# A stick-breaking mask moved from TensorE to VectorE, and an earlier release of an output copy, in a two-block transformer kernel

## The chip, the cores and the metric

The kernel runs on one core of a Trainium2 chip. The metric is the device time of one execution in microseconds. Below, the engines go by their names or by the profile's short forms: TensorE (PE; PEld is its weight load), VectorE (DVE), ScalarE (ACT), GpSimd (POOL), SyncE (SP).

## What is computed

A sequence of 512 tokens of width 1024 goes through two layers of a first block and then two layers of a second block, all in float32. The change lies in the second block, whose layer mixes four attention kinds: sliding window, latent (MLA), stick-breaking and forgetting (FoX) attention. The stick-breaking part of the reference, for which the mask is needed:

```python
z = jnp.einsum('bqhd,bkhd->bhqk', qi, k).astype(jnp.float32) * scale
strict = kpos[None, :] < qpos[:, None]
log_1mb = jnp.where(strict, jax.nn.log_sigmoid(-z), 0.0)
between = lax.cumsum(log_1mb, axis=3, reverse=True) - log_1mb
a = jnp.where(strict, jnp.exp(jax.nn.log_sigmoid(z) + between), 0.0)
return jnp.einsum('bhqk,bkhd->bqhd', a.astype(v.dtype), v)
```

After it each of the four groups is scaled by its root mean square and multiplied by the output weights:

```python
xf = mix.astype(jnp.float32).reshape(B, S, N_GROUPS, GROUP_WIDTH)
xf = xf * lax.rsqrt(jnp.mean(jnp.square(xf), axis=-1, keepdims=True) + eps)
y = _group_rmsnorm(mix, mix_g[l]) @ w_o[l]
```

## The kernel before

Every large product is made of three matmuls on numbers split into a high and a low part (mm3, L503 to L505), with moving tiles of 512 columns. Weights come from HBM in units of 128x1024; ScalarE casts the high part (L969), VectorE subtracts the low part (L977), both some units ahead of TensorE.

The attention of a layer of block 2 (tensor_block2, scalar_block2, vector_block2) runs in 32 steps. Step number 4a + j belongs to the pair of heads a (0 to 7) and its block j of 128 positions. The kinds are KIND = sliding window for a = 0, 1, latent for 2, 3, stick-breaking (SB) for 4, 5 and forgetting for 6, 7; so steps 16 to 23 are stick-breaking. A pair's two heads are m = 0 and 1. The order of the work is written out by hand, each engine with its own loop over the steps, and semaphores between them.

TensorE, step s: scores of s; weighted sum over V of step s-2; a filling of the projections' matmuls (nine at these steps); "between" of step s-1; a second filling; sometimes late work (a transpose of V or the sum of squares for a norm).

ScalarE, step s: copies of finished projections; sometimes a copy of V or the reciprocal root for a norm; the exponentials of s (softmax_exp, or sb_softplus for SB); the copy of the transposed probabilities of s-1, or for SB its weights (sb_weights); at j = 1 the output copy of pair a-1 (output_copy); casts of weights.

VectorE, step s: for SB the softplus sum and its high part of s, then splits of weights, then the splitting of the running sum (sb_split_sum, for SB steps with j > 0) and sum and low part (sb_add_and_low); at some steps a group norm; then, a step ahead of the sum of squares, add_and_split. At step 18 this is add_and_split for pairs 2 and 3 (L2450 to L2452), and at steps 20 and 21 group_norm(2) and group_norm(3) (L2349 to L2352), one pair each.

For one SB step with j > 0 the chain is: scores in two PSUM banks (L1869), the mask added there by an identity matmul over the 128 columns of the diagonal block (L1871), then on ScalarE Abs, Exp, Ln for m = 0 and again for m = 1 (L2115 to L2117). On VectorE follow max(z, 0) + Ln (L2394), the high part (L2414), the split of the running sum (L2422, L2425), the running sum and the low part (L2435, L2439); on TensorE in step s+1 the sums over later keys, added to the same banks (L1880 for j = 0, L1885 and L1888 else); on ScalarE the Exp that gives the weights (L2124); on TensorE in step s+2 the weighted sum (L1899). The widths grow with j: 128, 256, 384, 512 columns.

What waits for what around the change: the scores of an SB step from step 18 on wait for the weights of the step two before (bank_wait), because the banks alternate between two pairs; the same holds for the scores of step 24, which wait for the weights of step 22. The "between" of a step waits for the low parts. The weighted sum of a pair's first block waits for the output copy of the pair before (v_wait), which empties the PSUM bank O. The output copy of pair a writes into OUT_AT[a]; pairs 0, 2, 4 share one buffer and pairs 1, 3, 5 another:

```python
OUT_AT = (ext[0], ext[1], ext[0], ext[1], ext[0], ext[1], ext[3], rope_a)
```

The norm of pair t (group_norm(t)) reads OUT_AT[t] and raises y_ready to t + 1. For a in 2 to 5 the output copy waits until y_ready is 2 * (a // 2), that is 2, 2, 4, 4.

Of the kernel before, what the change touches and what calls it, by code (L numbers as in the profile page):

```python
# [35 lines left out]
SEQ = 512  # L36
# [62 lines left out]
class Steps:  # L99
# [10 lines left out]
    def wait(self, value=None):  # L110
# [8 lines left out]
TOTAL2 = {"unit_done": B2_UNITS, "tile_out0": MIX_TILES[0] + 22, "tile_out1": MIX_TILES[1] + 22,  # L119
          "tok_ready": 6 * (NB - 1), "tok_out": 6 * NB, "small_done": 5, "r_ready": 13, "r_out": 13, "rot_loaded0": 96, "rot_loaded1": 128, "gate_in": 1, "key_placed": 16, "stack_placed0": 112, "stack_placed1": 96, "rope_split": 2, "qk_ready": 2,  # L120
          "scores_ready": 48, "max_ready": 48, "probs_ready": 48, "probs_normed": 24, "t_ready": 48, "t_out": 48,
          "pv_done": 32, "o_out": 8, "sq_ready": 6, "sq_parts": 5, "rs_ready": 6, "y_ready": 8, "sb_scores": 16,
          "sb_ln": 16, "sb_sp": 16, "sb_cum": 16, "sb_sum": 12, "sb_prob": 16, "gate_ln": 1, "gate_ready": 1,
          "latent_ready": 3, "gu_ready": 22}

# [12 lines left out]
def program(nc, x_in, pos_in, const_in, mask_in, swa_in, rope2_in, col_in, w_in, row1_in,  # L138
            row2_in, out):
    ctx = ExitStack()  # L140
    with ctx:
# [4 lines left out]
        def sb(name, shape, dt=F32, at=None):  # L146

            size = 4
            for s in shape[1:]:
                size *= s  # L150
            offset = top[0] if at is None else at
            addr[name] = offset
            if at is None:
                top[0] += (size + 31) // 32 * 32
            return nc.alloc_sbuf_tensor_at(name, shape, dt, offset=offset)
# [21 lines left out]
        ident_r = sb("ident_r", [P, P], F32R)  # L177

        sbmask = sb("sbmask", [P, P])
        sbmask_r = sb("sbmask_r", [P, P], F32R, at=addr["sbmask"])  # L180

        causal = sb("causal", [P, SEQ])
        mult = sb("mult", [P, SEQ])
# [145 lines left out]
        gate_ready = sem("gate_ready")  # L329
        latent_ready = sem("latent_ready")  # L330
        sb_scores = sem("sb_scores")
        sb_ln = sem("sb_ln")
        sb_sp = sem("sb_sp")
        sb_cum = sem("sb_cum")
# [441 lines left out]
        def w_of(a, j):  # L776

            return 8 * (a - SB0) + 2 * j
# [694 lines left out]
        def vector_block1(dve, st, layer):  # L1473
# [41 lines left out]
            def fixed_tables():  # L1515
                st(nc.vector.tensor_copy(ident_r[:, :], ident))
                st.wait(st(nc.vector.memset(causal[:, 0:SEQ - P], 0.0)))
                st(nc.vector.tensor_copy(ones_r[:, :], ones))
                st(nc.vector.tensor_copy(tri_r[:, :], const[:, C_NTRI:C_NTRI + 2 * P]))
                dve.wait_ge(masks_loaded, 48)  # L1520
                st(nc.vector.tensor_copy(sbmask_r[:, :], sbmask[:, :]))

            if layer == 0:
                nc.vector.memset(ytmp[:, :], 0.0).then_inc(zeros_ready, 1)
# [212 lines left out]
        def tensor_block2(pe, layer):  # L1737
# [122 lines left out]
            def sb_scores_of(a, j):  # L1860

                lo = (NB - 1 - j) * P
                if j == 0:
                    operands_wait(a)
                bank_wait(a, j, 0)
                q, k, S = DEST[q_name(a)], DEST[k_name(a)], banks(a, j)
                for m in range(2):
                    rows = slice(HD * m, HD * m + HD)
                    nc.tensor.matmul(S[m][:, lo:SEQ], k[rows, lo:lo + P], q[rows, lo:SEQ], start=True, stop=False)  # L1869
                for m in range(2):  # L1870
                    nc.tensor.matmul(S[m][:, lo:lo + P], ident_r[:, :], sbmask_r[:, :], start=False, stop=True) \  # L1871
                      .then_inc(sb_scores, 1)

            def sb_between(a, j):
# [146 lines left out]
        def scalar_block2(act, st, layer):  # L2021
# [53 lines left out]
            def output_copy(a):  # L2075
                act.wait_ge(pv_done, at(pv_done, 4 * a + 4))
                if a in (2, 3, 4, 5):
                    act.wait_ge(y_ready, at(y_ready, 2 * (a // 2)))
                nc.scalar.activation(OUT_AT[a][:, :], O[:, :], ACT.Copy).then_inc(o_out, 1)
                if a % 2:  # L2080
                    act.wait_ge(o_out, at(o_out, a + 1))
                    if a == N_ATT - 1:
                        act.wait_ge(y_ready, at(y_ready, 6))
                    st(nc.scalar.activation(nrm[:, :], OUT_AT[a - 1][:, :], ACT.Square))
                    st.wait()
                    nc.scalar.activation(sq_tmp[:, :], OUT_AT[a][:, :], ACT.Square).then_inc(sq_parts, 1)
# [18 lines left out]
            def sb_softplus(a, j):  # L2105

                lo, w = (NB - 1 - j) * P, w_of(a, j)
                for m in range(2):
                    el = prob[m][:, lo:SEQ]
                    act.wait_ge(sb_scores, at(sb_scores, w + m + 1))  # L2110
                    if w == 0:
                        act.wait_ge(probs_normed, at(probs_normed, NB * SB0))
                    else:
                        act.wait_ge(sb_sp, at(sb_sp, w + m - 1))
                    st.wait(st(nc.scalar.activation(el, banks(a, j)[m][:, lo:SEQ], ACT.Abs)))  # L2115
                    st.wait(st(nc.scalar.activation(el, el, ACT.Exp, scale=-1.0)))
                    nc.scalar.activation(el, el, ACT.Ln, bias=1.0).then_inc(sb_ln, 1)  # L2117
# [147 lines left out]
        def vector_block2(dve, st, layer):  # L2265
# [107 lines left out]
            def gate_sums():  # L2373
# [9 lines left out]
                nc.vector.tensor_tensor(cum_r[32:36, :], cum, cum_r[0:4, :].bitcast(F32), ALU.subtract) \  # L2383
                  .then_inc(gate_ready, 1)

            def sb_softplus_sum(a, j):
                lo, w = (NB - 1 - j) * P, w_of(a, j)
                if w >= 4:
                    dve.wait_ge(sb_cum, at(sb_cum, w - 2))
                elif w == 2:  # L2390
                    dve.wait_ge(t_ready, at(t_ready, u_of(SB0 - 1, NB - 1, 1) + 1))
                for m in range(2):
                    dve.wait_ge(sb_ln, at(sb_ln, w + m + 1))
                    made = nc.vector.scalar_tensor_tensor(out=softplus_at(j)[m][:, lo:SEQ], in0=banks(a, j)[m][:, lo:SEQ],  # L2394
                                                          scalar=0.0, in1=prob[m][:, lo:SEQ], op0=ALU.max, op1=ALU.add)
                    if j:
                        softplus_step[m] = st(made)
                    else:
                        made.then_inc(sb_sp, 1)
# [60 lines left out]
            for step in range(STEPS):  # L2460
                a, qb = divmod(step, NB)
                late, made = LATE.get(step, ""), LATE.get(step - 1, "")
                ended = ENDS.get((step - 1, 1), [])
                if "kr" in ended:
                    gate_logits()
                if is_sb(step):
                    sb_softplus_sum(a, qb)
                    if qb:
                        sb_high(qb)
                elif step <= TAIL:  # L2470
                    row_max(a, qb, 0)
                    row_max(a, qb, 1)
                if LATE.get(step - 2) == "cq":
                    query_latents(1)
                for name in (*ENDS.get((step - 1, 0), []), *ended):
                    if step < TAIL:
                        next_split(name)
                if made == "cq":
                    normalise(a, qb)
                if is_sb(step) and qb == 0:  # L2480
                    sb_first_sum(a)
                elif is_sb(step):
                    sb_split_sum(a, qb)
                    sb_add_and_low(a, qb)
                if made == "cq":
                    dve.wait_ge(rs_ready, at(rs_ready, SQUARES["cq"]))
                    query_latents(0)
                elif made == "ckv":
                    dve.wait_ge(rs_ready, at(rs_ready, SQUARES["ckv"]))
                    scaled_split(ckv_t, colp[:, P2_GKV:P2_GKV + 1], z_t, 10, latent_ready, 3)  # L2490
                if ROTATE2.get(step - 1) == "kr":
                    rotate("kr", 0, z_t)
                elif ROTATE2.get(step - 1) == "qr":
                    rotate("qr", 1, qr_t)
                for tile, steps in ((0, 1), (1, 2)):
                    squared = LATE.get(step - steps, "")
                    if squared in ("e1", "e3"):
                        group_norm(int(squared[1]) - 1 + tile)
                if TAIL <= step < STEPS - 1:
                    row_max(N_ATT - 1, step + 1 - (STEPS - NB), 0)  # L2500
                    row_max(N_ATT - 1, step + 1 - (STEPS - NB), 1)
                if not is_sb(step) and made != "cq":
                    normalise(a, qb)
                if ROTATE2.get(step - 1) == "qr":
                    dve.wait_ge(qk_ready, at(qk_ready, 2))
                    split_query()
                elif ROTATE2.get(step - 2) == "qr":
                    split_key()
                if late == "cq":
                    add_squares("cq", *sz)  # L2510
                elif LATE.get(step + 1, "")[:1] == "e":
                    add_and_split(LATE[step + 1])
                if "kr" in ENDS[step, 0]:
                    gate_logits()
                if step == GATE_STEP + 1:
                    gate_sums()
                if step == TAIL:
                    split_to(dve, n0 + B2_WO + 2)
# [252 lines left out]
```

## Time and profile before

| | |
|---|---|
| median of 3 runs | 2381.99 us (2381.65 to 2382.66) |
| the profiled execution | 2382.52 us, span 2380.7 us, mean granted TensorE clock 0.998 |
| PE busy | 2360.4 us, 99% of the span, 11590 matmuls |
| PEld busy | 1906.1 us, 80% |
| DVE busy | 1301.2 us, 55% |
| ACT busy | 959.2 us, 40% |
| chain that ended last | PE 94%, DVE 3%, ACT 2%, issue 1%, DMA 1% |
| q1, the weights' DMA queue | 224.13 MB, 31.0% of 16 engines |

A busy share is a mean over the whole span; what a change is worth in one stretch is read from the timeline of that stretch. In a timeline's row the first number is the start in us, the second the duration in us (of several merged instructions up to the last one's end), then engine, line, operation, what it writes <- what it reads, sizes and count; in brackets the idle time of the engine just before it and what ended that. The stick-breaking steps lie at 1239 to 1301 us in layer 1 and at 1866 to 1927 us in layer 2. Matmuls are pipelined: the time that one takes in TensorE's queue is the distance to the next one's start, not its duration.

### The profile page before, as it was taken

The numbers are of one execution on the slowest core, as the hardware profiler recorded it, in microseconds if no ns is written. First come the engines' busy times: TensorE is split into PE (matmuls) and PEld (weight loads), VectorE is DVE, ScalarE is ACT, GpSimd is POOL, SyncE is SP. The second block draws the span as 40 slices with busy tenths as digits, with TensorE's granted clock in tenths as the row PEclk, the third lists the DMA queues.
The fourth block names the chain that finished last, engine by engine and source line by source line (L and its number), as shares of the span: only waits on it lengthen the run. The fifth ranks groups of instructions, "written<-read, shape, count | busy, mean of one in ns | idle before, by whom it ended". The sixth has DMA issues, their size and how long they took to land.

```text
span 2380.7 us, 29899 instructions
## 1 busy us (share of the span) xinstructions
PE 2360.4 (99%) x11590; PEld 1906.1 (80%) x11590; DVE 1301.2 (55%) x2404; ACT 959.2 (40%) x1763; POOL 0.2 (0%) x4
## 2 busy tenths in 40 slices
PE   9999999999999999999999999999999999999998
PEld 7888888888888888888766788888886768888887
DVE  6788763345588763335566553333356666333334
ACT  5356542224346642223566432222246664221222
POOL 0000000000000000000000000000000000000000
PEclk9999999999999999999999999999999999999999
DMA  4333333332344324333221223333323113333332
GB/s 172 106 103 108 97 104 90 97 114 67 99 118 108 101 76 132 97 97 106 69 71 47 97 88 94 96 96 97 114 71 86 54 36 107 106 97 97 98 97 89
DMA packets 73435, 226.30 MB, mean 95 GB/s; under 512 B 14096, under 2 KB 14992, under 8 KB 72528
## 3 DMA queue, kind: packets, MB, share of 16 engines
q1 hardware_dynamic: 73152, 224.13, 31.0%
q8 instruction: 93, 1.52, 0.3%
q14 instruction: 46, 0.38, 0.0%
q10 hardware_dynamic: 144, 0.26, 0.0%
HBM read 204.83 MB, written 2.10 MB: 87 GB/s over the span
## 4 chain that ended last, share of the span: by engine, by line
PE 94%; DVE 3%; ACT 2%; issue 1%; DMA 1%; DVEq 0%; ACTq 0%
PE bank L503 28%; PE bank L505 27%; PE bank L504 27%; PE bank L1129 2%; PE bank L1856 1%; PE bank L1815 1%; PE bank L1116 1%; PE bank L1840 1%; PE bank L1106 1%; PE bank L1104 1%; PE bank L443 1%; DVE x L493 1%; DMA raw_w<-w_dram 1%; ACT junk L478 0%; PE bank L1899 0%
## 5 line engine op out<-in xcount | busy, mean ns | idle before, releaser
L503 PE MATMUL bank<-h_hi,w_hi 128*128 128x512 f32 x1984 | 795.3, 401 | 1.4 <-ACT ks L2057 0.8
L505 PE MATMUL bank<-h_lo,w_hi 128*128 128x512 f32 x1984 | 775.2, 391 | 0.0
L504 PE MATMUL bank<-h_hi,w_lo 128*128 128x512 f32 x1984 | 773.8, 390 | 0.0
L977 DVE TENSOR_TENSOR w_lo<-raw_w,w_hi 128x1024 fp32r<-128x1024 f32 x358 | 431.2, 1222 | 207.3 <-ACT w_hi L969 203.9
L969 ACT ACTIVATE w_hi<-raw_w 128x1024 fp32r<-128x1024 f32 x358 | 375.0, 1055 | 339.4 <-DMA raw_w<-w_dram 339.0
L503 PEld LDWEIGHTS bank<-h_hi,w_hi 128*128 128x128 f32 x1984 | 372.9, 188 | 91.0 <-issue 18.1
L505 PEld LDWEIGHTS bank<-h_lo,w_hi 128*128 128x128 f32 x1984 | 372.6, 188 | 80.6
L504 PEld LDWEIGHTS bank<-h_hi,w_lo 128*128 128x128 f32 x1984 | 373.5, 188 | 70.4 <-issue 0.2
L503 PE MATMUL bank<-w_hi,act_hi 128*128 128x512 f32 x480 | 188.5, 393 | 0.0
L2544 DVE TENSOR_TENSOR ytmp<-nrm,bank 128x512 f32<-128x512 f32 x44 | 30.3, 688 | 287.5 <-PE bank L505 287.5
L505 PE MATMUL bank<-w_lo,act_hi 128*128 128x512 f32 x480 | 186.9, 389 | 0.0
L504 PE MATMUL bank<-w_hi,act_lo 128*128 128x512 f32 x480 | 186.9, 389 | 0.0
L1418 ACT ACTIVATE ext<-bank 128x512 f32<-128x512 f32 x48 | 28.8, 599 | 278.8 <-PE bank L505 278.8
L2212 ACT ACTIVATE nrm<-bank 128x512 f32<-128x512 f32 x44 | 26.4, 599 | 257.2 <-PE bank L505 257.2
L1717 DVE TENSOR_TENSOR rope_a<-ext,bank 128x512 f32<-128x512 f32 x32 | 22.0, 687 | 160.7 <-PE bank L505 107.3
L503 PEld LDWEIGHTS bank<-w_hi,act_hi 128*128 128x128 f32 x480 | 90.1, 188 | 19.5 <-issue 1.4
L505 PEld LDWEIGHTS bank<-w_lo,act_hi 128*128 128x128 f32 x480 | 90.1, 188 | 18.9
L504 PEld LDWEIGHTS bank<-w_hi,act_lo 128*128 128x128 f32 x480 | 90.2, 188 | 18.2
L1362 ACT ACTIVATE prob<-prob,small 128x128 f32<-128x128 f32 (+3 forms) x128 | 70.9, 556 | 55.7 <-DVE small L679 55.7
L503 PE MATMUL bank<-act_hi,w_hi 128*128 128x512 f32 x212 | 83.3, 393 | 0.0
L505 PE MATMUL bank<-act_lo,w_hi 128*128 128x512 f32 x212 | 82.6, 390 | 0.0
L504 PE MATMUL bank<-act_hi,w_lo 128*128 128x512 f32 x212 | 82.5, 389 | 0.0
(335 smaller groups left out, 2775.4 us busy)
## 6 DMA issues: line engine op xcount, KB each, us to landing
raw_w<-w_dram SPq DMA_DIRECT2D x356, 512.0 KB, 3.6
extra_raw<-w_dram SPq DMA_DIRECT2D x10, 512.0 KB, 4.6
k_lo<-k_lo SPq DMA_DIRECT2D x32, 128.0 KB, 2.4
ln_row<-row_dram SPq DMA_DIRECT2D x4, 1024.0 KB, 5.8
x<-x_dram SPq DMA_DIRECT2D x4, 512.0 KB, 6.9
rowp<-row_dram SPq DMA_DIRECT2D x2, 1024.0 KB, 9.7
rot_t<-raw_t SPq DMA_DIRECT2D x128, 16.0 KB
act_hi<-q_lo SPq DMA_DIRECT2D x16, 128.0 KB, 2.3
```

Source lines behind the costliest of these rows:

```text
L443: last = nc.tensor.transpose(entry_banks(e, tb)[half][:, k * P:(k + 1) * P], src[:, (4 * half + k) * P:(4 * half + k + 1) * P], ident)
L493: return nc.vector.scalar_tensor_tensor(out=x[:, tb, cols], in0=hn[tb][:, cols], scalar=small[:, 20 + tb:21 + tb], in1=ln_row[:, D:2 * D][ ...
L503: nc.tensor.matmul(dst, lh, rh, start=start, stop=False)
L504: nc.tensor.matmul(dst, ll, rh, start=False, stop=False)
L505: return nc.tensor.matmul(dst, lh, rl, start=False, stop=stop)
L969: nc.scalar.activation(hi_of(u), raw_of(u), ACT.Copy).then_inc(hi_cast, 1)
L977: nc.vector.tensor_tensor(lo_of(u), raw_of(u), hi_of(u).bitcast(F32), ALU.subtract) \
L1129: last = nc.tensor.matmul(O[rows, cols], vs[a % 2][:, b, rows], pT[ti1(a, qb, m) % 2][:, b * P:(b + 1) * P], start=(b == 0), stop=(b == qb))
L1362: nc.scalar.activation(prob[m][:, 0:nk], prob[m][:, 0:nk], ACT.Exp, scale=-1.0, bias=small[:, 24 + 2 * qb + m:25 + 2 * qb + m], accum_out= ...
L1418: nc.scalar.activation(ext[i][:, :], gate_bank(mm, i)[:, :], ACT.Sigmoid).then_inc(tile_out[0], 1)
L2212: nc.scalar.activation(nrm[:, :], PT[0][:, :], ACT.Silu).then_inc(tile_out[0], 1)
L2544: nc.vector.tensor_tensor(ytmp[:, :], nrm[:, :], PT[1][:, :], ALU.mult).then_inc(tile_out[1], 1)
```

## The change

Three edits belong together. TensorE no longer adds the mask: the score matmul ends its group itself and signals. VectorE adds the mask in the PSUM bank (sb_mask), at the head of its step, in front of the softplus sum, and signals by a new semaphore, sb_masked; ScalarE's Abs waits for that instead of for the scores. And the output copy of pair a waits until y_ready is a - 1 instead of 2 * (a // 2): 1, 2, 3, 4 for a = 2 to 5 instead of 2, 2, 4, 4. The rounded copy of the mask, made once at the start, goes, since no matmul reads it; a wait for the steps before it takes its place.

```diff
@@ fixed_tables
                 dve.wait_ge(masks_loaded, 48)
-                st(nc.vector.tensor_copy(sbmask_r[:, :], sbmask[:, :]))
+                st.wait()
@@ sb_scores_of
                 for m in range(2):
                     rows = slice(HD * m, HD * m + HD)
-                    nc.tensor.matmul(S[m][:, lo:SEQ], k[rows, lo:lo + P], q[rows, lo:SEQ], start=True, stop=False)
-                for m in range(2):
-                    nc.tensor.matmul(S[m][:, lo:lo + P], ident_r[:, :], sbmask_r[:, :], start=False, stop=True) \
+                    nc.tensor.matmul(S[m][:, lo:SEQ], k[rows, lo:lo + P], q[rows, lo:SEQ], start=True, stop=True) \
                       .then_inc(sb_scores, 1)
@@ output_copy
                 if a in (2, 3, 4, 5):
-                    act.wait_ge(y_ready, at(y_ready, 2 * (a // 2)))
+                    act.wait_ge(y_ready, at(y_ready, a - 1))
@@ sb_softplus
-                    act.wait_ge(sb_scores, at(sb_scores, w + m + 1))
+                    act.wait_ge(sb_masked, at(sb_masked, w + m + 1))
@@ vector_block2
+            def sb_mask(a, j):
+                own, w = slice((NB - 1 - j) * P, (NB - j) * P), w_of(a, j)
+                for m in range(2):
+                    dve.wait_ge(sb_scores, at(sb_scores, w + m + 1))
+                    bank = banks(a, j)[m][:, own]
+                    nc.vector.tensor_tensor(bank, bank, sbmask[:, :], ALU.add).then_inc(sb_masked, 1)
@@ vector_block2, loop over the steps
                 if is_sb(step):
+                    sb_mask(a, qb)
                     sb_softplus_sum(a, qb)
                     if qb:
                         sb_high(qb)
```

## Rows read from the trace of the kernel before

**Rows 1.** Waits of TensorE: who waited <- for whom, us in total, times, longest
```profile
PE bank L1899 <- issue: 4.6, 2, 2.3
```

**Rows 2.** Timeline of TensorE, step 21: start us, us, engine, line, operation
```profile
1276.49 0.44 PE L1871 MATMUL bank<-sbmask_r,ident_r 128*128 128x128 f32 x2
...
1276.86 1.08 PE L1899 MATMUL bank<-pT,vs 128*64 128x512 f32 x4
```

**Rows 3.** Timeline of all engines, layer 1, around step 22: the same columns
```profile
1284.71 0.69 DVE L2352 TENSOR_TENSOR act_lo<-ytmp,act_hi 128x512 fp32r<-128x512 f32 x1
...
1285.50 0.60 ACT L2079 ACTIVATE ext<-bank 128x512 f32<-128x512 f32 x1 [4.54 <-DVE act_lo L2352]
...
1286.20 0.29 PE L1899 MATMUL bank<-z_t,vs 128*64 128x128 f32 x1 [2.28 <-issue]
```

**Rows 4.** Windows behind that wait, both layers: busy (x), granted clock PEclk
```profile
1287.20:1290.60 3.40, 3.40 (x12) 2.72 (x10) 0.61 (x2) 3.19 (x7) 0.00 (x0) 0.50 0.00 0
1913.55:1917.00 3.45, 3.45 (x22) 2.89 (x22) 0.49 (x1) 3.35 (x7) 0.00 (x0) 1.00 0.00 0
```

**Rows 5.** Timeline of ScalarE, layer 1: first Abs of steps 17 to 20
```profile
1247.20 0.38 ACT L2115 ACTIVATE prob<-bank 128x256 f32<-128x256 f32 x1 [0.71 <-PE bank L1871]
...
1254.53 0.48 ACT L2115 ACTIVATE prob<-bank 128x384 f32<-128x384 f32 x1
...
1262.11 0.60 ACT L2115 ACTIVATE prob<-bank 128x512 f32<-128x512 f32 x1 [1.12 <-DVE sp_low L2439]
...
1269.57 0.26 ACT L2115 ACTIVATE prob<-bank 128x128 f32<-128x128 f32 x1
```

**Rows 6.** Timeline of VectorE, steps 17 to 22: second L2394, end of step
```profile
1249.68 0.43 DVE L2394 SCALAR_TENSOR_TENSOR pn<-bank,prob 128x256 f32<-128x256 f32 x1 [0.68 <-ACT prob L2117]
...
1253.48 0.43 DVE L2439 TENSOR_TENSOR sp_low<-pn,act_hi 128x256 fp32r<-128x256 f32 x1
...
1257.65 0.56 DVE L2394 SCALAR_TENSOR_TENSOR ext<-bank,prob 128x384 f32<-128x384 f32 x1 [0.86 <-ACT prob L2117]
...
1264.17 0.69 DVE L2452 TENSOR_TENSOR sq_lo<-nrm,sq_hi 128x512 fp32r<-128x512 f32 x1
1264.78 0.69 DVE L2394 SCALAR_TENSOR_TENSOR pn<-bank,prob 128x512 f32<-128x512 f32 x1
...
1265.89 0.69 DVE L2394 SCALAR_TENSOR_TENSOR pn<-bank,prob 128x512 f32<-128x512 f32 x1 [0.42 <-ACT prob L2117]
...
1268.64 1.28 DVE L2439 TENSOR_TENSOR sp_low<-pn,act_hi 128x512 fp32r<-128x512 f32 x2
...
1271.55 0.29 DVE L2394 SCALAR_TENSOR_TENSOR ext<-bank,prob 128x128 f32<-128x128 f32 x1 [0.64 <-ACT prob L2117]
...
1275.09 0.69 DVE L2352 TENSOR_TENSOR act_lo<-ytmp,act_hi 128x512 fp32r<-128x512 f32 x1
...
1279.34 0.43 DVE L2394 SCALAR_TENSOR_TENSOR pn<-bank,prob 128x256 f32<-128x256 f32 x1 [0.65 <-ACT prob L2117]
...
1290.55 0.56 DVE L2394 SCALAR_TENSOR_TENSOR ext<-bank,prob 128x384 f32<-128x384 f32 x1 [0.83 <-ACT prob L2117]
...
1295.41 0.56 DVE L2439 TENSOR_TENSOR sp_low<-ext,act_hi 128x384 fp32r<-128x384 f32 x1
```

**Rows 7.** Timelines: weights (ScalarE); scores of steps 17, 20, 24 (TensorE)
```profile
1246.20 0.70 PE L1869 MATMUL bank<-wq_t,wk_t 64*128 64x256 f32 x4
...
1266.61 0.50 ACT L2124 ACTIVATE qr_t<-bank 128x384 f32<-128x384 f32 x1
...
1268.30 0.49 PE L1869 MATMUL bank<-cq_t,ckv_t 64*128 64x128 f32 x4
...
1301.40 0.49 PE L1815 MATMUL bank<-ks,qs 64*128 64x128 f32 x4
...
1873.54 0.70 PE L1869 MATMUL bank<-wq_t,wk_t 64*128 64x256 f32 x4
...
1927.49 0.49 PE L1815 MATMUL bank<-ks,qs 64*128 64x128 f32 x4 [0.24 <-ACT qr_t L2124]
```

More of the change, by code:

```diff
@@ L121 @@
           "scores_ready": 48, "max_ready": 48, "probs_ready": 48, "probs_normed": 24, "t_ready": 48, "t_out": 48,
-          "pv_done": 32, "o_out": 8, "sq_ready": 6, "sq_parts": 5, "rs_ready": 6, "y_ready": 8, "sb_scores": 16,
+          "pv_done": 32, "o_out": 8, "sq_ready": 6, "sq_parts": 5, "rs_ready": 6, "y_ready": 8, "sb_scores": 16, "sb_masked": 16,
           "sb_ln": 16, "sb_sp": 16, "sb_cum": 16, "sb_sum": 12, "sb_prob": 16, "gate_ln": 1, "gate_ready": 1,
@@ L179, in program @@
         sbmask = sb("sbmask", [P, P])
-        sbmask_r = sb("sbmask_r", [P, P], F32R, at=addr["sbmask"])
         causal = sb("causal", [P, SEQ])
@@ L331, in program @@
         sb_scores = sem("sb_scores")
+        sb_masked = sem("sb_masked")
         sb_ln = sem("sb_ln")
```

## The prediction

> **What bounds the kernel now.** I read the waits of TensorE first, then the stretch of the stick-breaking heads in order of time. TensorE is busy for nearly the whole span, so only two things count: work taken from its queue, and the few places where it stands still. The longest of these is the first weighted sum of the second pair of stick-breaking heads, 4.6 us in two waits, one in each layer [rows 1]. Below I number the steps as the code does (step = 4a + j): the stick-breaking pairs are a = 4 and 5, steps 16 to 23, and the reader should hold on to four points of each step: TensorE's scores (L1869), ScalarE's first Abs (L2115), VectorE's second softplus sum (L2394), and the last thing that VectorE does in the step.
>
> **Part 1: the mask matmuls go.** Each step has two, and from the start of the first to the start of what follows is 1276.86 - 1276.49 = 0.37 us of TensorE's queue [rows 2]. There are 16 pairs (8 steps, 2 layers): 16 x 0.37 = 5.9 us. The other matmuls keep their number and shapes. One fixed copy of the mask at the start also goes from VectorE; it lies beside the loads at the start and I cost it at nothing (0.3 us at most, that of a 128x128 operation [rows 6]).
>
> **Part 2: the output copy of pair 4 waits for norm 2, no longer for norm 3.** Of the four copies only those of pairs 2 and 4 get a lower count; for pairs 3 and 5 the new formula gives the old value. Today VectorE ends norm 3 at 1285.40, ScalarE copies at 1285.50, and TensorE goes on at 1286.20, after 2.28 us of idleness [rows 3]. Norm 2 ends at 1275.78 [rows 6], long before, so the copy can start as soon as ScalarE comes to it, and this wait goes: both of them are 4.6 us [rows 1]. In layer 1 the idleness was also followed by 3.4 us at a granted clock of 0.50, the lower (1.2 GHz) of its two levels; after the equal wait of layer 2 the clock stayed at 1.00 [rows 4]. Half of 3.4 is 1.7 us lost in the profiled run. Pair 2's copy frees nothing: TensorE shows no wait there [rows 1].
>
> Together that would be 5.9 + 4.6 + 1.7 = 12.2 us, if nothing else moved.
>
> **Part 3: VectorE adds the mask, and ScalarE now waits for VectorE.** The additions are cheap: 32 operations of 128x128, each like the softplus sum of that size, which also reads a PSUM bank: 0.29 us [rows 6]. None in the trace writes PSUM from VectorE, so the bounds are 0.2 (a saving against that row if the start overlaps) and 0.45; I take 0.29 since its inputs and size are the same. The Trainium skill's page "Perfetto Trace Analysis", section "Optimizing Scalar/DVE Operations", puts VectorE's access overhead at about 60 ns on SBUF and 125 ns on PSUM; if the store to PSUM costs that difference again, each addition takes 0.36 and the sum below grows by 12 x 0.07 = 0.8 us. No run here shows it.
>
> What matters is the place in the queue. The additions of step s stand in front of the softplus sums of step s, therefore behind everything of step s-1: splits of sums and softplus, and at steps 18, 20 and 21 the squares and the norms too. ScalarE's Abs, Exp and Ln of step s wait for them, and behind these in ScalarE's queue stand the weights of step s-1, for which TensorE's scores of step s+1 wait. No DMA is issued by any of this, but the tile copies and casts behind the Abs on ScalarE move later with it; their users come a whole tile of weights later, so I cost them at nothing.
>
> Today ScalarE works on step s while VectorE still ends step s-1: at step 19 the Abs starts at 1262.11, VectorE is at work until 1264.86 [rows 5, 6]. That overlap is forbidden by the change. In its place stands a ring: addition (VectorE), Abs to Ln of both heads (ScalarE), rest of the step (VectorE), next addition. The Trainium skill's page "TensorE: Matmul & The Clock Gate", section "Architectural detail: the array is 16× 32×32, not 1× 128×128", calls VectorE's and ScalarE's queues strictly first in, first out, which speaks against this change; could an addition pass the norm in the queue, the sum would stay near the 12.2 us.
>
> One lap of the ring is A + T + 0.31. A is from the first Abs to the second softplus sum, T from there to the end of VectorE's step, and 0.31 is the addition (0.29), 0.10 from VectorE's end to ScalarE's start (1285.40 to 1285.50 [rows 3]), less 0.08, by which dense VectorE instructions overlap (L2452 ends at 1264.86, the next starts at 1264.78 [rows 6]). From [rows 5, 6], and [rows 3] for the end of step 21:
> step 17: 2.48 + 4.23 + 0.31 = 7.0
> step 18: 3.12 + 7.21 + 0.31 = 10.6
> step 19: 3.78 + 4.03 + 0.31 = 8.1
> step 20: 1.98 + 4.23 + 0.31 = 6.5
> step 21: 2.48 (as step 17, same width) + 6.06 + 0.31 = 8.9
> step 22: 3.12 (as step 18) + 5.42 + 0.31 = 8.9
> Sum 50.0 us. The ring starts with the Abs of step 17, 1.00 us after its scores (1246.20 to 1247.20), as today: the first addition takes the place of the mask matmul. It ends for TensorE with the scores of step 24 (L1815), which wait for the weights of step 22: from the Abs of a step of 512 columns to the end of the weights of the step before is 1267.11 - 1262.11 = 5.0 (step 19; step 23 has the same widths), and 0.1 more to TensorE [rows 3, 5, 7]. So from the scores of step 17 to those of step 24: 1.0 + 50.0 + 5.0 + 0.1 = 56.1 us.
>
> Today that stretch is 55.20 us in layer 1 and 53.95 in layer 2 [rows 7]. TensorE alone would need 55.2 - 2.3 - 1.7 - 7 x 0.37 = 48.6. So it would wait 7.5 us in each layer, in new places. The scores of step 20 are first: by TensorE alone 22.10 - 3 x 0.37 = 21.0 us after those of step 17 [rows 7], by the ring 1.0 + 7.0 + 10.6 + 5.0 + 0.1 = 23.7, a wait of 2.7 us; the other 4.8 lie before the scores of steps 23 and 24. VectorE then stands about 1 us later behind the scores of step 24 than today; I take it that the softmax heads after it hide this, and it costs up to 1 us per layer if they don't.
>
> **The sum.** Layer 1: 56.1 - 55.2 = +0.9, less 0.37 for step 16, which lies outside the stretch: +0.5. Layer 2: 56.1 - 53.95 - 0.37 = +1.8. Together +2.3 us. The 1.7 us of low clock in layer 1 are inside the 55.2 and so already given back. But the change makes six waits of some 2 to 3 us where there were two of 2.3, one of which was followed by the low clock. A fall behind the waits of steps 20 and 23 costs nothing, since TensorE then waits less at the next; one behind the last wait of a layer costs 1.7. Of two such I take one, as today: +1.7. In all +4.0 us. On the profiled execution's own 2382.52 (span 2380.7 and 1.8 around it) that is 2386.5; the median of the runs is 0.5 lower, so I predict 2386.0.
>
> **Rivals.** (a) The ring has a hole and the direct sum counts: 2382.0 - 12.2 = 2369.8 us. For it speaks that VectorE isn't full: it stands idle for 0.42 to 0.86 us before its second sums [rows 6]. Against it: this is waiting for ScalarE's Ln, inside the ring, and stands in A already. A ring shorter by 0.5 us in each of twelve laps would still only give -2. (b) Slower: TensorE waits before step 24 in both layers, the clock falls behind both, and the additions cost up to 0.45 (12 x 0.16 = 1.9). It gives +2.3 + 3.4 = 5.7 up to 7.6: 2387.7 to 2389.6. It decides from a second fall, or from 0.06 us more per lap beyond the forecast. For it speaks that the new waits are as long as the one that was followed by the low clock, or longer. (c) The clock never falls there: 2384.3, within my forecast's band. (d) The lower count does nothing, since norm 2 is late as well. By the code norms 0, 1 and 2 make the count of 3, so this needs norm 2 to slip by a step; then the copy stands inside lap 21 with its 0.60 us [rows 3] in each layer, which adds 1.2 us to the forecast and is part of (b).
>
> **How the numbers follow.** About 0.2% (4.8 us) is what a measurement of this kernel can tell from no change. Forecast, ring with none or one fall, -2 to +4.8 us: 0.48. (b), slower: 0.40. (a), faster by over 4.8 us, in full or in half: 0.12. The range leaves (a) out and takes in the bounds of the addition on both sides: below, additions of 0.2 and no fall, +2.3 - 1.1 = +1.2, and 0.3 us less in each lap for overlaps that I didn't see, to -2; above, (b) with 1 us of passed-on delay: 2380 to 2391.
>
> **What would show it.** No idle time before L1899 for pair 5's first block, 0.37 us less per step, ScalarE's Abs waiting for VectorE at steps 19 to 23 of both layers, and TensorE waiting for ScalarE's weights (L2124) before the scores of steps 20, 23 and 24, some 7.5 us per layer; scores 17 to 24 in 56 us. VectorE's additions should read about 0.29 us. The prediction is wrong if the Abs of step 19 starts before the split of the squares of pairs 2 and 3 (L2452) has ended, if that stretch takes under 52 us, or if waits after step 24 show the delay handed on.

## The result and the profile after

Timed beside each other in 20 runs each, the kernel before has a median of 2381.73 us (2380.26 to 2383.15) and the changed kernel 2387.16 us (2384.60 to 2391.85). The ratio is 1.0025, with a 95% interval of 1.0019 to 1.0031 (the two medians divided give 1.0023): slower by 5.4 us. That is clear of no change, but the interval still takes in the 0.2% that the prediction used as its line. The profiled execution took 2385.67 us, 3.15 us more than that of before; it is the fifth fastest of the 20, so the traces show less of the loss than the medians do.

The page of the changed kernel, its first lines (busy us, share of the span, instructions):

```profile
span 2383.9 us, 29871 instructions
## 1 busy us (share of the span) xinstructions
PE 2357.7 (99%) x11558; PEld 1902.6 (80%) x11558; DVE 1308.7 (55%) x2435; ACT 957.9 (40%) x1763; POOL 0.2 (0%) x4
```

TensorE has its 32 matmuls less (11590 to 11558) and VectorE its 31 operations more, and still the span is longer. The waits of TensorE say where the gain went (who waited <- for whom, us in total, times, longest):

```profile
PE bank L1869 <- ACT qr_t L2122: 5.4, 2, 2.7
PE bank L1815 <- ACT qr_t L2122: 4.8, 2, 2.4
PE bank L1869 <- ACT pT L2122: 1.7, 2, 1.4
PE bank L1883 <- DVE sp_low L2444: 0.4, 2, 0.2
```

The wait of [rows 1], 4.6 us for the output copy, isn't among them. In its place stand three waits in each layer, all for the stick-breaking weights of ScalarE: before the scores of step 20, of step 23 and of step 24, together 11.9 us in both layers, and a small one for the low parts.

The additions themselves (one line's instructions: shortest/median/longest ns; then who waited for them):

```profile
L2389 DVE TENSOR_TENSOR bank<-bank,sbmask x32: 287/292/300, 1238.5 to 1923.8; 128x128 f32<-128x128 f32 x32
...
  ACT prob L2113: 31.4, 14
```

They take 0.29 us each, as the softplus sum of that size did [rows 6]. But ScalarE stood idle for 31.4 us in all before Abs operations that waited for them. Step 19 of layer 1, against [rows 5, 6] of before, is the place to see it (VectorE, then ScalarE, then TensorE, each in order of time):

```profile
1261.80 0.69 DVE L2457 TENSOR_TENSOR sq_lo<-nrm,sq_hi 128x512 fp32r<-128x512 f32 x1
1262.40 0.49 DVE L2389 TENSOR_TENSOR bank<-bank,sbmask 128x128 f32<-128x128 f32 x2
...
1266.50 0.69 DVE L2399 SCALAR_TENSOR_TENSOR pn<-bank,prob 128x512 f32<-128x512 f32 x1 [1.05 <-ACT prob L2115]
```

```profile
1262.73 0.60 ACT L2113 ACTIVATE prob<-bank 128x512 f32<-128x512 f32 x1 [4.57 <-DVE bank L2389]
...
1267.22 0.49 ACT L2122 ACTIVATE qr_t<-bank 128x384 f32<-128x384 f32 x1
```

```profile
1267.85 0.80 PE L1869 MATMUL bank<-cq_t,ckv_t 64*128 64x128 f32 x4 [2.69 <-ACT qr_t L2122]
```

The scores of step 19 were issued at 1257.46. VectorE came to the additions only at 1262.40, straight behind the split of the squares; ScalarE had been idle for 4.57 us and began at 1262.73; its weights of step 18 ended at 1267.71, and TensorE, which had stood since 1265.2, went on with the scores of step 20 at 1267.85.

### The profile page after: what moved, and what is told of

It is laid out like the page before. It is cut to its first block, busy times and chain, and to the rows that moved or that the text cites. A ratio compares the mean times of both kernels' runs of the same rounds, so it can differ in the third digit from the quotient of the medians.

```text
span 2383.9 us, 29871 instructions
## 1 busy us (share of the span) xinstructions
PE 2357.7 (99%) x11558; PEld 1902.6 (80%) x11558; DVE 1308.7 (55%) x2435; ACT 957.9 (40%) x1763; POOL 0.2 (0%) x4
## 4 chain that ended last, share of the span: by engine, by line
PE 91%; DVE 4%; ACT 3%; issue 1%; DMA 1%; DVEq 0%; ACTq 0%
PE bank L503 27%; PE bank L505 26%; PE bank L504 26%; PE bank L1129 2%; PE bank L1856 1%; PE bank L1815 1%; PE bank L1116 1%; PE bank L1840 1%; PE bank L1106 1%; PE bank L1104 1%; PE bank L443 1%; DVE x L493 1%; DVE w_lo L977 1%; DMA raw_w<-w_dram 1%; ACT prob L2114 0%
```

## Experiments

All of them ran beside the kernel before, whose median was 2381.7 in both sets. "Stretch" is again the time from the scores of step 17 to those of step 24, in layers 1 and 2: 55.20 and 53.95 us before, 56.47 and 55.96 us in the changed kernel.

### The copy's lower count alone (e1)

```diff
@@ output_copy, kernel before
-                    act.wait_ge(y_ready, at(y_ready, 2 * (a // 2)))
+                    act.wait_ge(y_ready, at(y_ready, a - 1))
```

> Only the output copy's lower count, the mask stays on TensorE. Ring theory (the additions close a ring of VectorE and ScalarE; the copy's count by itself is a plain gain): the two idle stretches of 2.3 us before pair 5's first weighted sum go, and with them the clock's fall behind one of them; about 2376.3 us, 5.5 below before, no wait of TensorE over 1 us in steps 16 to 24. Rival (the copy's early release is what upsets ScalarE's order and costs the time): at or above before, 2382 us or more.

Measured: 2374.74 us (2373.53 to 2375.75), ratio 0.9970 (0.9960 to 0.9981); stretch 51.30 us in both layers. The copy's count is a plain gain of 7.0 us, 1.5 more than expected. In the profiled run no low clock is left in the stretch, and TensorE has no wait for the copy and none of over 0.15 us from step 16 to the scores of step 24. So the part that was forecast as a gain is one, and the whole loss of the change stands against 2374.7, not against 2381.7: the mask's move costs 12.4 us.

### The mask's move alone (e2)

```diff
@@ output_copy, changed kernel
-                    act.wait_ge(y_ready, at(y_ready, a - 1))
+                    act.wait_ge(y_ready, at(y_ready, 2 * (a // 2)))
```

> Only the mask moves to VectorE, the output copy of pair 4 waits for norm 3 as before. Ring theory: the copy, a tile copy and a cast then stand between norm 3 and the Abs of step 22, so lap 21 grows by 1.6 us in each layer: about 2390.4 us. Rival (the parts add up, each by itself): the changed kernel's 2387.2 plus the 4.6 to 5.5 us that the copy's count gives alone, 2392 us. Rival (the mask's move is a gain of 5.9 us and the copy's count a loss): 2376 us.

Measured: 2387.83 us (2385.16 to 2392.59), ratio 1.0028 (1.0019 to 1.0038); stretch 58.07 and 57.61 us. This is a miss by 2.6 us, and an instructive one. The stretch did grow by 1.6 us in each layer, as the ring theory says, but the time by only 0.7. The waits and the windows behind two of them (granted clock third from the end) show what gave it back in the profiled run:

```profile
PE bank L1897 <- issue: 7.3, 2, 4.2
PE bank L1869 <- ACT qr_t L2122: 5.4, 2, 2.7
```

```profile
1287.80:1291.10 3.30, 3.30 (x11) 2.72 (x11) 0.86 (x2) 2.89 (x7) 0.00 (x0) 0.50 0.00 0
1301.60:1305.00 3.40, 3.40 (x18) 2.31 (x19) 3.23 (x12) 1.01 (x2) 0.00 (x0) 1.00 0.02 5
```

The long wait now stands at the weighted sum of step 22, in the middle of the ring, and the clock falls to 0.50 behind it, where TensorE has time to lose. The wait before step 24 is down to 0.24 and 0.26 us, and the clock behind it stays at 1.00. In the changed kernel it fell there in both layers:

```profile
1302.10:1305.40 3.30, 3.30 (x9) 2.48 (x8) 2.90 (x8) 0.88 (x4) 0.00 (x0) 0.50 0.00 0
...
1930.10:1933.40 3.30, 3.30 (x9) 1.84 (x6) 3.13 (x8) 0.88 (x4) 0.00 (x0) 0.50 0.00 0
```

From the scores of step 24 to the next wait of TensorE (its L1856 matmuls after the last step) it took 33.68 us in both layers before, 35.22 and 35.25 in the changed kernel, and 33.67 here in layer 1: the fall behind the last wait costs 1.5 to 1.6 us each time. The rival that adds the parts up (2392) falls: under the ring, the copy's count that is worth 7.0 us alone is worth 0.7, which is inside the spread of either kernel's runs and can't be told from nothing. The traced run is the fastest of its ten (2385.16), and five of the others took 2389 us or more at a lower mean clock; where the clock fell in those isn't recorded, so this account holds for the traced run and isn't shown for the median.

### Only the dependence (e8)

```diff
@@ kernel before, with the copy's lower count
+            def sb_mask(a, j):
+                w = w_of(a, j)
+                for m in range(2):
+                    dve.wait_ge(sb_scores, at(sb_scores, w + m + 1))
+                    nc.vector.memset(ytmp[:, m:m + 1], 0.0).then_inc(sb_masked, 1)
@@ sb_softplus
-                    act.wait_ge(sb_scores, at(sb_scores, w + m + 1))
+                    act.wait_ge(sb_masked, at(sb_masked, w + m + 1))
@@ loop over the steps
                 if is_sb(step):
+                    sb_mask(a, qb)
                     sb_softplus_sum(a, qb)
```

> The mask stays on TensorE, the copy has the lower count, and only the dependence is made: VectorE writes one column of a scratch buffer at the place of each addition, and ScalarE's Abs waits for that. Ring theory: the order alone costs the time; a lap is some 0.23 us shorter than with the additions, step 16 keeps its 0.37: about 2385 us, with waits of over 2 us before scores 20 and 24. Rival (the additions' duration or their writes to PSUM cost it): 2374.7 us, as with the lower count alone.

Measured: 2385.57 us (2382.84 to 2387.65), ratio 1.0015 (1.0007 to 1.0024); stretch 56.63 us in both layers. Its waits of TensorE, and the one-column fills (the lines stand one lower than in the kernel before):

```profile
PE bank L1816 <- ACT qr_t L2125: 3.9, 2, 1.9
PE bank L1870 <- ACT qr_t L2125: 3.4, 2, 1.7
```

```profile
L2391 DVE MEMSET ytmp<- x32: 59/59/59, 1239.2 to 1924.8; 128x1 f32 x32
...
  ACT prob L2116: 24.7, 14
```

Nothing is moved from TensorE and VectorE's work is 59 ns per fill, and 10.8 us are lost against the copy's count alone. It is the order, not the additions or their writes to PSUM. (The waits are 1.7 and 1.9 us, not over 2 as expected, because TensorE still has the mask to add in that time.) One thing came out differently: the stretch isn't shorter than with the real additions. The clock fell in both layers, 1.6 to 1.9 us after the end of the wait before step 20, TensorE then took 9.12 us instead of 7.56 to the scores of step 21, and VectorE stood idle for 1.27 and 1.41 us before the fill of step 21, waiting for them. So a fall in the middle of the ring isn't always free: here it cost some 1.3 us in each layer (an estimate: the lap of step 20 took 7.59 us, against the changed kernel's undisturbed 6.45 less the 0.2 by which a fill is shorter than an addition).

### A longer ring (e5)

```diff
@@ sb_mask, changed kernel
                     bank = banks(a, j)[m][:, own]
+                    if m == 0:
+                        st.wait(st(nc.vector.memset(ytmp[:, :], 0.0)))
```

> The changed kernel with one more operation in each lap: VectorE fills a 128x512 scratch buffer with zeros ahead of the first addition of every step and waits for its end (the fill of 384 columns took 0.38 us, so 0.5 here, with the wait 0.55). Ring theory: 12 laps x 0.55 = 6.5 us more than the changed kernel, about 2393.5 us. Rival (VectorE has room, its added work is hidden, the cost of the change is elsewhere): 2387.2 us.

Measured: 2397.55 us (2396.76 to 2398.24), ratio 1.0067 (1.0054 to 1.0079); stretch 61.45 and 60.57 us.

```profile
L2390 DVE MEMSET ytmp<- x16: 485/485/485, 1240.0 to 1933.7; 128x512 f32 x16
```

```profile
PE bank L1869 <- ACT qr_t L2122: 8.7, 2, 4.4
PE bank L1815 <- ACT qr_t L2122: 6.1, 2, 3.1
```

The ring passes everything on: 10.4 us, where hidden work would have cost none. The expected 6.5 was too low in two places. A lap grew by 0.65 us (VectorE's step 19 from the second sum to the first addition: 4.61 instead of 3.95), since at this place the instructions no longer overlap (at step 20 the fill begins 0.06 us behind the end of the one ahead, the addition 0.04 behind the end of the fill, where the addition had begun 0.08 before its forerunner's end); and it is seven fills to a stretch, that of step 17 too: 7 x 0.65 = 4.6, which is what layer 2's stretch grew by (60.57 - 55.96). Between the two profiled runs the difference is 11.9 us: the two stretches hold 9.6 of it, and behind the last wait of layer 2 the low clock lasted 6.8 us instead of 3.4, which cost 1.2 more.

### The additions ahead of squares and norms (e3)

```diff
@@ loop over the steps, changed kernel
                 if is_sb(step):
-                    sb_mask(a, qb)
+                    if step == NB * SB0:
+                        sb_mask(a, qb)
                     sb_softplus_sum(a, qb)
...
                 elif is_sb(step):
                     sb_split_sum(a, qb)
                     sb_add_and_low(a, qb)
+                if is_sb(step) and is_sb(step + 1):
+                    sb_mask(*divmod(step + 1, NB))
```

> The changed kernel, with the additions of step s+1 issued in step s right behind the sums and low parts, ahead of the squares and norms (steps 18, 20, 21 get shorter laps: 8.9, 4.7, 7.0 instead of 10.6, 6.5, 8.9). Ring theory: stretch from scores 17 to 24 about 51 us instead of 56, one wait of 1 us before scores 20 and one before scores 24; about 2374.8 us. Rival (the additions themselves cost the time, by what VectorE's writes to PSUM or its occupation slow): about 2387 us as before the move, since their number is the same.

Measured: 2373.05 us (2372.28 to 2373.98), ratio 0.9963 (0.9950 to 0.9975); stretch 51.12 and 51.11 us, 0.9 and 1.3 us of waiting in the expected places, no low clock in the stretch. The time is 1.7 us under the expectation.

```profile
PE bank L1815 <- ACT qr_t L2122: 2.7, 2, 1.3
PE bank L1869 <- ACT qr_t L2122: 1.8, 2, 0.9
```

The same 32 additions, put in VectorE's queue ahead of three pieces of work instead of behind them, and the kernel is 14.1 us faster.

### The additions ahead of the low parts too (e4)

```diff
@@ loop over the steps, on top of e3's first edit
                 if is_sb(step) and qb == 0:
                     sb_first_sum(a)
+                    sb_mask(*divmod(step + 1, NB))
                 elif is_sb(step):
                     sb_split_sum(a, qb)
+                    if is_sb(step + 1):
+                        sb_mask(*divmod(step + 1, NB))
                     sb_add_and_low(a, qb)
```

> The changed kernel, with the additions of step s+1 issued in step s ahead of the running sums and low parts (all laps under TensorE's own time per step). Ring theory: TensorE no longer waits at scores 20, 23 and 24, the direct sum comes true: 5.9 for the mask matmuls, 4.6 for the two idle stretches, 0.9 for the clock on the mean: about 2370.4 us. Rival (the additions themselves cost it): about 2387 us.

Measured: 2372.05 us (2371.50 to 2373.31), ratio 0.9960 (0.9948 to 0.9973); stretch 50.93 and 50.94 us. Expected was 2370.4: waits of 0.71 us before the scores of step 20 and 1.15 before those of step 24 stayed. Step 19 shows why (VectorE, then ScalarE):

```profile
1259.32 0.49 DVE L2389 TENSOR_TENSOR bank<-bank,sbmask 128x128 f32<-128x128 f32 x2
...
1260.31 0.56 DVE L2444 TENSOR_TENSOR sp_low<-rope_a,act_hi 128x384 fp32r<-128x384 f32 x1
```

```profile
1260.96 0.60 ACT L2113 ACTIVATE prob<-bank 128x512 f32<-128x512 f32 x1 [2.68 <-DVE sp_low L2444]
```

The additions are done at 1259.81, and the Abs starts at 1260.96, behind the low part of step 18. That wait was there all the time: it keeps ScalarE from overwriting the buffer that VectorE's softplus sum of the step before reads, and the low part was the next signal behind it. In the kernel before, too, the Abs of step 19 came out of it ([rows 5], the row that starts at 1262.11, 1.12 us). Now it closes a second ring.

### The same, without that wait (e7)

```diff
@@ sb_softplus, on top of e4
                     if w == 0:
                         act.wait_ge(probs_normed, at(probs_normed, NB * SB0))
-                    else:
-                        act.wait_ge(sb_sp, at(sb_sp, w + m - 1))
```

> The kernel with the additions ahead of the running sums and low parts, in which ScalarE's Abs also drops its wait for the low part of the step before (the wait for the additions, which come behind the reading of that buffer, covers it). Theory: that wait closed a second ring, through the low part, which left waits of 0.71 us before scores 20 and 1.15 before scores 24 in each layer; both go: 2372.05 - 3.7 = 2368.3 us, stretch from scores 17 to 24 about 49.1 us. Rival (those waits come from the additions' own time on VectorE): 2372 us.

Measured: 2367.76 us (2367.39 to 2368.81), ratio 0.9941 (0.9928 to 0.9955); stretch 48.73 and 48.71 us. TensorE waits nowhere from step 16 to step 24, and ScalarE's Abs follows the additions (the additions of step 19, then the Abs):

```profile
1260.08 0.50 DVE L2387 TENSOR_TENSOR bank<-bank,sbmask 128x128 f32<-128x128 f32 x2
```

```profile
1260.41 0.60 ACT L2111 ACTIVATE prob<-bank 128x512 f32<-128x512 f32 x1 [0.79 <-DVE bank L2387]
```

This version beats both kernels: by 14.0 us the one before, by 19.4 the changed one. Its stretch confirms the 48.6 us that the prediction had put down for TensorE alone.

### No mask at all (e6)

```diff
@@ sb_softplus, changed kernel
-                    act.wait_ge(sb_masked, at(sb_masked, w + m + 1))
+                    act.wait_ge(sb_scores, at(sb_scores, w + m + 1))
@@ loop over the steps
                 if is_sb(step):
-                    sb_mask(a, qb)
                     sb_softplus_sum(a, qb)
```

> The changed kernel without the addition of the mask: no engine adds it, and ScalarE's Abs waits for TensorE's scores alone. The output leaves the stick-breaking mask out. Ring theory: without the additions' place in VectorE's queue the ring is open and the gain of the other edits shows: 5.9 + 4.6 + 0.9, less up to 1 us for a wait of the Abs for the low parts of the step before: 2370.4 to 2371.5 us. Rival (the loss comes from TensorE's shorter steps or the copy's early release): 2380 us or more.

Measured: 2368.73 us (2368.09 to 2369.56), ratio 0.9946 (0.9934 to 0.9958); stretch 48.89 and 48.90 us, 1.7 us under the lower expectation. It is 18.4 us faster than the changed kernel, and 6.0 faster than e1, from which it differs by TensorE's 16 x 0.37 = 5.9 us. e7, with the additions in it, is no slower (1.0 us faster, with ranges that overlap), so the additions as such cost nothing that can be seen here; e7 also lacks the wait for the low part, so the two aren't a clean pair.

## Why the prediction was right

**The time.** Forecast 2386.0, range 2380 to 2391; measured 2387.16, so +5.4 us against a forecast of +4.0. The likeliest case was named "within 0.2%" with 0.48 and "slower" with 0.40; the measured 5.4 us lies on the slower side of that line, 0.5 us short of the rival (b), with both clock falls that (b) names. So the case that was held likeliest isn't the one that came, by 0.6 us; the range and the mechanism held.

**Parts 1 and 2, each by itself.** 5.9 us for the mask matmuls is confirmed by e6 against e1 (6.0). For the copy 4.6 us and 1.7 of clock were named for the profiled run; e1 gave 7.0 on the medians, and 3.90 and 2.65 us in the stretches (55.20 and 53.95 to 51.30).

**The ring.** This is the step on which the sign hung, and it held lap by lap. Forecast for steps 17 to 22: 7.0, 10.6, 8.1, 6.5, 8.9, 8.9. From Abs to Abs the changed kernel took 6.96, 10.59, 8.05, 6.96, 8.92, 8.80 us in layer 1 and 6.96, 10.59, 8.06, 6.45, 8.93, 8.79 in layer 2. At step 19 the scores had been issued at 1257.46, and the addition began at 1262.40, behind all that stood ahead of it in VectorE's queue; it passed nothing. The stretch was forecast at 56.1 and took 56.47 and 55.96. The 0.5 us more at step 20 in layer 1 are a clock fall: the additions of step 21 waited for TensorE's scores. That the order and not the addition does it is shown three ways: e8 (order without additions, 2385.6), e3 (additions without that order, 2373.1), and e5 (each added piece of a lap arrives in full).

**The waits.** Their places were right: scores of steps 20, 23, 24. Their sum was forecast at 7.5 us per layer and is 5.6 in layer 1 and 6.7 in layer 2; of the "six waits of some 2 to 3 us" only four are so long. The first was forecast at 2.7 us and measured at 2.69 and 2.70. Before step 24 it was 2.4 in both, before step 23 0.33 and 1.37, and 0.20 and 0.21 before the sums of step 22. That the clock's fall behind step 20 eats into the next waits is seen in layer 1, where the wait of step 23 is 1.0 us shorter than in layer 2.

**The term that was too small** is the clock. One fall was taken behind the two last waits, and the profiled run had both, 1.5 to 1.6 us each. Of the 3.15 us by which the profiled runs differ, the steps 16 to 24 hold 0.97 + 1.73 = 2.7 (forecast 2.3) and the 33 us behind them 1.54 + 1.57 = 3.1 (forecast 1.7); the parts of the program in front of layer 1's and layer 2's step 16 took 1.8 and 0.9 us less than before. How much of the 1.8 us is the edit's isn't shown: in the five kernels whose code is the same up to there (the changed one, e3, e4, e5, e7) step 16 of layer 1 begins anywhere from 1237.58, the changed kernel's, to 1239.02 us. So it is partly luck that the profiled run landed at 2385.67, under the 2386.5 forecast for it: with the start of before it would have been 2387.5. The claim that a fall behind the waits of steps 20 and 23 costs nothing was too strong, by 0.5 us here and by some 1.3 per layer in e8. The spread fits: of the 20 runs of the changed kernel those with a mean granted clock of 0.998 took 2384.6 to 2385.4 us, those with 0.993 to 0.995 2388.9 to 2391.9. The median lies 1.5 us above the profiled run, and the runs beside it show a mean clock of 0.996 against its 0.997, so they had more time at the low clock than the trace shows; where, isn't recorded. By contrast e3, e4 and e7, without a wait over 1.4 us in the stretch, spread over 1.8 us at most in their five runs each, and e1, which has none either, over 2.2 us in seven.

**Handed-on delay.** Not seen: in e2 and e3, where the clock didn't fall there, layer 1 took 33.67 us from the scores of step 24 to the next wait, as before.

**Left open.** The 0.9 us that layer 2 gained in front of its step 16 are a shorter wait of TensorE in the steps of the earlier kinds, 1.04 us before and 0.12 after. In the changed kernel's list only layer 1's is left:

```profile
PE bank L1815 <- ACT wq_t L2055: 0.5, 1, 0.5
```

In all kernels in which VectorE adds the mask this wait of layer 2 is 0.1 us, in e1, e6 and e8 it is 0.6 to 0.8. Why isn't known. Nor was it tried what makes the clock fall behind one wait and not behind an equal one.

## What to carry to other kernels

Before a step is moved to an engine that has room on the mean, write down what stands ahead of it in that engine's queue, and whether the engine that waits for the result feeds this one: if so, two engines that had overlapped take turns, and the lap (own work, the other's work, everything queued between) is to be compared with the bound engine's time for the same step. Moving cheap work off the critical engine and putting it right for the queue are one edit: here, against the copy's lower count alone, the same 32 additions cost 12.4 us behind the norms and gained 1.7 in front of them, and 7.0 once they stood in front of the low parts too and a wait on a convenient later signal was dropped. A freed wait is worth only what the next constraint leaves of it: the copy's count gave 7.0 us by itself and 0.7, within the noise, under the ring.

## What the runs showed of the hardware

Where idleness stands matters as much as how long it is, through the clock. TensorE idle for 2.4 to 2.7 us was followed by the lower clock level in three of four such waits of the changed kernel's profiled run, and waits of up to 1.34 us (e3) never were. Length alone doesn't decide it: in e8 the waits of 1.7 us before step 20 were followed by it in both layers and the longer ones of 1.9 before step 24 were not. The price depends on the place: 1.5 to 1.6 us behind the last wait of the chain, where nothing absorbs it, and in the middle 0.5 in the changed kernel and some 1.3 in e8. VectorE's addition with one source and the destination in PSUM took 0.292 us, no more than the sum that only reads PSUM (0.29), and 7 ns more than a subtraction of the same 128x128 size with nothing in PSUM (L2430, 0.285). From the Trainium skill's page "Perfetto Trace Analysis", section "Optimizing Scalar/DVE Operations", one could have estimated 65 ns more for a second access to PSUM (125 less 60 ns). That doesn't show in the duration here.
